# First stage of a one-core diffusion backbone step: six column chunks instead of four, its last block run in the main loop

## The chip, the cores and the metric

The kernel runs on one core of one Trainium2 chip. The metric is the device time of one execution, in microseconds (us), lower is better. Engines: TensorE (PE, matmuls; PEld is its weight load), VectorE (DVE), ScalarE (ACT), GpSimd (POOL) and SyncE (SP, which only issues DMAs here). A dense matmul's 512 columns can start every 0.23 us at TensorE's upper clock and every 0.43 us at half of it.

## What is computed

One layer over 128 context tokens and 128 latent tokens (streams s = 0 and 1), model width 2048, float32:

```python
mods = silu(c) @ w_ada + b_ada            # shift1, scale1, gate1, shift2, scale2, gate2, per stream
h = rmsnorm(x, norm1_g) * (1 + scale1) + shift1
p = h @ w_in + b_in                       # u_fourier (1024) | q | k | v (1024 each) | gate_A | gate_B (2048 each)
a = fourier_mix(p.u_fourier) @ w_fourier
b = attention(p.q, p.k, p.v, cached keys and values, bias) @ w_na_o     # 8 heads of 128
x = x + gate1 * ((sigmoid(p.gate_A) * a + sigmoid(p.gate_B) * b) @ w_out)
h2 = rmsnorm(x, norm2_g) * (1 + scale2) + shift2
x = x + gate2 * hier_moe(h2)              # 16 experts of hidden width 512, two per token
y = rmsnorm(x, final_norm_g)              # also returned: k and v of the context tokens
```

## The kernel before

**Dense steps.** All dense weights stream in 96 steps `l` of 1 MB each (512 rows by 512 columns: LOAD_K = 4 slices of 128 rows). Such a load goes into a ring `raw` of four slots. ScalarE rounds it to `w_hi` (`high`, L1309) and VectorE takes the rest, `w_lo` (`low`, L1663), in two half loads, called units. Each unit is 12 matmuls on TensorE (`unit`, L759 to L761: hi by hi, hi by lo, lo by hi, two row slices, two streams). There are four slots of `w_hi`/`w_lo` (AHEAD = 4 units), so the conversion of a unit waits until the unit four before it has been used, and a ring slot comes free when both of its halves have been converted.

**adaLN rows.** `w_ada` is 96 MB. The shift1 and scale1 columns (32 MB) are taken in four blocks of 512 columns. A block is eight loads of 1 MB into a ring `araw` of four slots, each used by one `ada_block` (16 matmuls, L722). When the eight are in, ScalarE copies the sums to `modrow` (`evac_block_rows`, L1361), TensorE turns them (`mod_block`, L777), VectorE finishes `mod` (L1713, L1715), and both modulate and split four slices of h (`modulate`, `split_h`, `h_ready`). The other four vectors (64 MB) come as 64 "supers" through the ring `raw`, each used by one `ada_super` (L738). SP issues all these loads from one queue, in the order of use; a load that waits for its slot holds up everything behind it.

**First stage.** A slice of h is ready only after its adaLN block. So steps 0 to 15 run block by block: block b of four applies the rows of h that it has just got to P0_CHUNKS = 4 column chunks of `w_in`, and VectorE adds each result to the sum in SBUF (`add_partial`, L1745). Between the units TensorE runs the next block's `ada_block`s: two after unit 0, one after 1, two after 2, one after 3, two after 4, then half of unit 5, `mod_block`, the other half, and units 6 and 7. In the last block it runs supers 0 to 4 there. ScalarE, in program order, does `high` of the next block's first unit, then `evac_block_rows`, then `modulate`.

**Main loop.** Steps 16 to 95: the other four chunks of q, k, v and u (to L_MERGE = 32), the gates with `w_na_o` and `w_fourier` (to L_OUT = 80), and `w_out`. One super runs in each step after its first unit, up to step 69; the last five come at the end. Beside them run the eight attention heads, one every two steps from step 17 (HEAD_AT): `head_transposes` (L862, L865) at HEAD_AT, `scores` (L871 to L873) one step later, `transpose_probs` (L881) two and `probs_values` three steps later. The transposes of a head's cached keys wait until VectorE has scaled the scores of the head before (`scale_scores`, L1893 to L1899, `scores_ready`), since both use PSUM bank 6. The cached keys and values have two slots in `cst`: POOL loads head h when head h - 2 is done. POOL loads the attention bias (written to DRAM and read back skewed), and the DFT constants, once all four blocks of h are ready (`h_ready` 8).

**Experts.** After step 95 come routing and the 16 experts, 192 MB of weights in a ring of eleven slots; a first few of these loads start as the dense ring comes free.

## Time and profile before

| | |
|---|---|
| Median of 3 runs | 1247.66 us (1242.78, 1247.66, 1248.76) |
| The profiled execution's own time | 1242.94 us |
| Its span | 1241.1 us |
| TensorE busy | 1151.5 us, 93% |
| DMA | 424.33 MB, mean 342 GB/s |

The profile is of one execution. Its rows are given below in groups. Times in them are us from the start of the span, so a row's place can be compared with the stages: the first adaLN block up to 40.9 us, the four blocks of the first stage up to about 176.5 us, the main loop up to about 745 us, routing and experts to the end. A matmul's duration is modelled to its end and overlaps the next one's start; the steps between starts tell the pace.

### The profile page before, as it was taken

The numbers are of one execution on the slowest core, as the hardware profiler recorded it, in microseconds if no ns is written. First come the engines' busy times: TensorE is split into PE (matmuls) and PEld (weight loads), VectorE is DVE, ScalarE is ACT, GpSimd is POOL, SyncE is SP. The second block draws the span as 40 slices with busy tenths as digits, with TensorE's granted clock in tenths as the row PEclk, the third lists the DMA queues.
The fourth block names the chain that finished last, engine by engine and source line by source line (L and its number), as shares of the span: only waits on it lengthen the run. The fifth ranks groups of instructions, "written<-read, shape, count | busy, mean of one in ns | idle before, by whom it ended". The sixth has DMA issues, their size and how long they took to land.

```text
span 1241.1 us, 14456 instructions
## 1 busy us (share of the span) xinstructions
PE 1151.5 (93%) x5593; PEld 685.3 (55%) x5593; DVE 529.9 (43%) x760; ACT 368.6 (30%) x516; POOL 45.4 (4%) x83
## 2 busy tenths in 40 slices
PE   4899989999999999999999999999998989888785
PEld 2556657776756666767887774444343334333232
DVE  0355545555434445455565546125233232414046
ACT  3323323443333333333445534222011011201013
POOL 0000210010000300000000000000000000000000
PEclk9899999999999999999999999999999999999998
DMA  9999898887767998888675559999999999999998
GB/s 358 387 383 383 306 356 313 286 315 274 257 212 273 302 335 318 313 314 306 201 251 188 203 191 424 395 423 423 422 423 424 423 424 422 422 423 424 423 413 344
DMA packets 114404, 424.33 MB, mean 342 GB/s; under 512 B 8912, under 2 KB 9088, under 8 KB 81440
## 3 DMA queue, kind: packets, MB, share of 16 engines
q1 hardware_dynamic: 109600, 411.59, 86.5%
q0 software_dynamic: 4144, 11.22, 2.7%
q8 instruction: 45, 0.74, 0.2%
q10 hardware_dynamic: 592, 0.59, 0.1%
q14 instruction: 23, 0.19, 0.0%
HBM read 419.42 MB, written 3.95 MB: 341 GB/s over the span
## 4 chain that ended last, share of the span: by engine, by line
PE 68%; DMA 28%; DVE 1%; issue 1%; SPq 1%; ACT 1%; POOL 0%; DVEq 0%
PE bank L759 14%; PE bank L761 13%; PE bank L760 13%; PE bank L1138 10%; DMA mraw<-in_w_exp_up 6%; PE bank L738 4%; DMA raw<-in_w_in 3%; DMA mraw<-in_w_exp_gate 3%; PE bank L1168 3%; DMA raw<-in_w_ada 2%; PE bank L1079 2%; DMA araw<-in_w_ada 2%; DMA mraw_y<-in_w_exp_gate 2%; DMA mraw_g<-in_w_exp_up 2%; DMA mraw_x<-in_w_exp_up 2%; DMA mraw_g<-in_w_exp_down 2%
## 5 line engine op out<-in xcount | busy, mean ns | idle before, releaser
L1663 DVE TENSOR_TENSOR w_lo<-raw,w_hi 128x1024 fp32r<-128x1024 f32 x192 | 233.7, 1224 | 268.4 <-ACT w_hi L1309 268.0
L1309 ACT ACTIVATE w_hi<-raw 128x1024 fp32r<-128x1024 f32 x192 | 202.2, 1058 | 323.8 <-PE bank L761 233.0
L759 PE MATMUL bank<-w_hi,h_hi 128*128 128x512 f32 x512 | 212.5, 415 | 2.5 <-DVE w_lo L1663 2.5
L1138 PE MATMUL bank<-mraw,xg 128*64 128x512 f32 x768 | 193.6, 602 | 15.8 <-DMA mraw<-in_w_exp_gate 7.8
L761 PE MATMUL bank<-w_hi,h_lo 128*128 128x512 f32 x512 | 202.4, 395 | 0.0
L760 PE MATMUL bank<-w_lo,h_hi 128*128 128x512 f32 x512 | 202.3, 395 | 0.0
L1138 PEld LDWEIGHTS bank<-mraw,xg 128*64 128x64 f32 x768 | 61.8, 137 | 118.2 <-issue 113.9
L759 PEld LDWEIGHTS bank<-w_hi,h_hi 128*128 128x128 f32 x512 | 97.8, 191 | 53.0 <-issue 34.7
L761 PEld LDWEIGHTS bank<-w_hi,h_lo 128*128 128x128 f32 x512 | 97.5, 190 | 21.8
L760 PEld LDWEIGHTS bank<-w_lo,h_hi 128*128 128x128 f32 x512 | 97.8, 191 | 19.3 <-issue 1.0
L1168 PE MATMUL bank<-mraw,hidT 128*64 128x512 f32 x320 | 83.3, 596 | 16.1 <-DMA mraw<-in_w_exp_down 13.7
L2104 DVE SCALAR_TENSOR_TENSOR d_lo<-bank,slot_w,d_hi 128x512 fp32r<-128x512 f32 x32 | 24.0, 748 | 160.5 <-ACT d_hi L1609 159.8
L1609 ACT ACTIVATE d_hi<-bank,slot_w 128x512 fp32r<-128x512 f32 x32 | 22.0, 687 | 229.6 <-PE bank L1168 142.2
L2116 DVE TENSOR_TENSOR bank<-bank,ga2b 128x512 f32<-128x512 f32 x64 | 41.5, 694 | 79.6 <-PE bank L1209 79.5
L738 PE MATMUL bank<-raw,cpad 128*32 128x512 f32 x512 | 68.0, 604 | 5.6 <-DMA raw<-in_w_ada 5.6
L1168 PEld LDWEIGHTS bank<-mraw,hidT 128*64 128x64 f32 x320 | 26.7, 136 | 60.4 <-issue 56.0
L722 PE MATMUL bank<-araw,cpad 128*32 128x512 f32 x256 | 34.8, 640 | 18.7 <-DMA araw<-in_w_ada 18.7
L759 PE MATMUL bank<-w_hi,m_hi 128*128 128x512 f32 x128 | 51.5, 402 | 0.0
L761 PE MATMUL bank<-w_hi,m_lo 128*128 128x512 f32 x128 | 50.0, 391 | 0.0
L760 PE MATMUL bank<-w_lo,m_hi 128*128 128x512 f32 x128 | 49.9, 390 | 0.0
L2051 DVE TENSOR_TENSOR xg<-bank,rbi 128x512 f32<-128x512 f32 x32 | 21.9, 686 | 53.0 <-PE bank L1079 52.5
L1138 PE MATMUL bank<-mraw_x,xg 128*64 128x512 f32 x88 | 40.0, 597 | 2.1 <-DMA mraw_y<-in_w_exp_gate 1.7
(277 smaller groups left out, 1305.0 us busy)
## 6 DMA issues: line engine op xcount, KB each, us to landing
raw<-in_w_in SPq DMA_DIRECT2D x64, 1024.0 KB, 5.6
raw<-in_w_ada SPq DMA_DIRECT2D x64, 1024.0 KB, 7.3
mraw<-in_w_exp_up SPq DMA_DIRECT2D x51, 1024.0 KB, 20.9
mraw<-in_w_exp_gate SPq DMA_DIRECT2D x49, 1024.0 KB, 20.9
mraw<-in_w_exp_down SPq DMA_DIRECT2D x40, 1024.0 KB, 20.8
araw<-in_w_ada SPq DMA_DIRECT2D x64, 512.0 KB, 10.0
raw<-in_w_out SPq DMA_DIRECT2D x16, 1024.0 KB, 5.1
raw<-in_w_na_o SPq DMA_DIRECT2D x8, 1024.0 KB, 5.2
```

The source lines that it names most:

```text
L722: last = nc.tensor.matmul(bank[7 - b % 2][32 * g:32 * g + 32], cpad[:, 2 * j + g % 2], araw[:, n % ARAW, g], start=j == 0, stop=j == 7)
L738: last = nc.tensor.matmul(bank[7][32 * g:32 * g + 32], cpad[:, k], raw[:, n % RAW, g], start=k == 0, stop=k == KD - 1)
L759: nc.tensor.matmul(o, hi[:, k, s], wh, start=k == first, stop=False)
L760: nc.tensor.matmul(o, hi[:, k, s], wl, start=False, stop=False)
L761: last = nc.tensor.matmul(o, lo[:, k, s], wh, start=False, stop=k == final)
L1079: last = nc.tensor.matmul(out[:, kk * EPG * CAP:(kk + 1) * EPG * CAP], (t_hi, t_lo)[part][:, s, k * P:(k + 1) * P], pick[:, s, g * EPG:(g ...
L1138: last = nc.tensor.matmul(out[x * CAP:(x + 1) * CAP], xg[:, q * LOAD_K + kk, e * CAP:(e + 1) * CAP], slab(slot)[:, kk * COL:(kk + 1) * COL ...
L1168: last = nc.tensor.matmul(bank[first_bank + n][x * CAP:(x + 1) * CAP], hidT[:, i % 2, k, x * CAP:(x + 1) * CAP], slab(slot)[:, n * COL:(n ...
L1309: nc.scalar.activation(w_hi[:, u % AHEAD], r, ACT.Copy).then_inc(hi_ready, 1)
L1663: v.tensor_tensor(w_lo[:, u % AHEAD], r, w_hi[:, u % AHEAD].bitcast(F32), ALU.subtract).then_inc(raw_done[n % RAW], 4)
L2104: v.scalar_tensor_tensor(out=d_lo[:, c % 2], in0=bank[first_bank + n][:], scalar=slot_w[:, i:i + 1], in1=d_hi[:, c % 2].bitcast(F32), op0= ...
L2116: v.tensor_tensor(bank[out + s][:], bank[out + s][:], ga2b[:, s, cols], ALU.mult).then_inc(y_scaled, 1)
```

## The change

P0_CHUNKS goes from 4 to 6, so that q, k and v are all in the first stage. Only three of its blocks (steps 0 to 17) stay in the block loop; the fourth (steps 18 to 23) is run by the main loop, which now starts at L_LOOP = 18 and also carries the supers from super 0 on: two in step 18, then one in each step up to step 76. L_MERGE, L_OUT and L_ALL stay 32, 80 and 96. In the block loop one `ada_block` follows each of the units 0 to 7 of a block's twelve, and `mod_block` stands behind unit 8. In SP's order the super loads stand one step further ahead of the dense loads, and are used with a lead of one step in the new numbering. The heads start at steps 21, 23, 24, 26, 28, 29, 31 and 33, `cst` has four slots, ScalarE's exponentials wait for the transposes of the head before, and POOL loads four heads and six bias rows first, then the attention bias once three blocks of h are ready.

```diff
@@ -200,3 +200,3 @@
         mb = place("mb", [P, NS, COL], B + 4 * KB)
-        cst = place("cst", [P, 2, 2, HD], B + 8 * KB)
+        cst = place("cst", [P, 4, 2, HD], B + 4 * KB)
         qkT = place("qkT", [P, 4, TOK], B + 10 * KB)
@@ -333,3 +333,4 @@
-        P0_CHUNKS, BLOCKS = 4, 4
+        P0_CHUNKS, BLOCKS = 6, 4
+        L_LOOP = P0_CHUNKS * (BLOCKS - 1)
         L_MAIN = 4 * P0_CHUNKS
@@ -339,4 +340,3 @@
         A_SUPER = 32
-        A_MAIN = A_SUPER + 3
-        L_LAST_ADA = L_MAIN + 96 - A_MAIN
+        L_LAST_ADA = L_LOOP + 96 - A_SUPER
         LATE_ADA = 5
@@ -345,5 +345,5 @@
-        ring_order = ["dense"] * (L_MAIN - 3) + ["ada", "dense"] * 3
-        for l in range(L_MAIN, L_ALL):
-            ring_order += ["ada", "dense"] if l < L_LAST_ADA - LATE_ADA else ["dense"]
+        ring_order = ["dense"] * (L_LOOP + 1)
+        for l in range(L_LOOP, L_ALL):
+            ring_order += ["ada"] * (l < L_LAST_ADA - LATE_ADA) + ["dense"] * (l + 1 < L_ALL)
         ring_order += ["ada"] * LATE_ADA
@@ -363,3 +363,3 @@
-        ADA_LEAD = 2
+        ADA_LEAD = 1
@@ -367,3 +367,8 @@
-            return L_MAIN + 16 * (super_chunk - GATE1) + 15 + A_SUPER - A_MAIN - ADA_LEAD
+            return L_LOOP + 16 * (super_chunk - GATE1) + 15 - ADA_LEAD
+
+        def supers_at(l):
+
+            first, last = l + ADA_LEAD * (l > L_LOOP), l + ADA_LEAD
+            return [A_SUPER + i - L_LOOP for i in range(first, last + 1) if i < L_LAST_ADA - LATE_ADA]
@@ -395,3 +400,3 @@
-        HEAD_AT = [L_MAIN + 1 + 2 * h for h in range(8)]
+        HEAD_AT = [L_LOOP + i for i in (3, 5, 6, 8, 10, 11, 13, 15)]
         DFT_AT = HEAD_AT[7] + 2
@@ -485,13 +490,12 @@
             for b in range(1, BLOCKS):
-                for i in range(4):
-                    ada_block_load(b, 2 * i)
-                    ada_block_load(b, 2 * i + 1)
+                for i in range(P0_CHUNKS):
+                    if i < 4:
+                        ada_block_load(b, 2 * i)
+                        ada_block_load(b, 2 * i + 1)
                     dense_load(P0_CHUNKS * (b - 1) + i + 1)
-            for i in range(3):
-                ada_super_load(A_SUPER + i)
-                dense_load(L_MAIN - 3 + i)
-            for l in range(L_MAIN, L_ALL):
+            for l in range(L_LOOP, L_ALL):
                 if l < L_LAST_ADA - LATE_ADA:
-                    ada_super_load(A_MAIN + l - L_MAIN)
-                dense_load(l)
+                    ada_super_load(A_SUPER + l - L_LOOP)
+                if l + 1 < L_ALL:
+                    dense_load(l + 1)
@@ -633,6 +637,6 @@
-                if h >= 2:
-                    pool.wait_ge(pv_done, h - 1)
-                pool.dma_start(cst[:, h % 2, 0:1], kc_v[:, h:h + 1, :]).then_inc(ctx_landed[h % 2], 16)
-                pool.dma_start(cst[:, h % 2, 1:2], vc_v[:, h:h + 1, :]).then_inc(ctx_landed[h % 2], 16)
+                if h >= 4:
+                    pool.wait_ge(pv_done, h - 3)
+                pool.dma_start(cst[:, h % 4, 0:1], kc_v[:, h:h + 1, :]).then_inc(ctx_landed[h % 4], 16)
+                pool.dma_start(cst[:, h % 4, 1:2], vc_v[:, h:h + 1, :]).then_inc(ctx_landed[h % 4], 16)
@@ -645,10 +649,10 @@
             pool.wait_ge(xT_ready, 6)
-            load_bin(0)
-            load_bin(1)
-            load_bin(2)
-            load_bin(3)
-            pool.wait_ge(h_ready, 8)
-            load_bias_rows()
             load_cached_head(0)
             load_cached_head(1)
+            load_cached_head(2)
+            load_cached_head(3)
+            for n in range(6):
+                load_bin(n)
+            pool.wait_ge(h_ready, 6)
+            load_bias_rows()
             skew_bias_rows()
@@ -656,9 +660,3 @@
             pool.dma_start(cst_all[:, C_DFTN:C_MASK], constants[:, C_DFTN:C_MASK]).then_inc(consts_in, 16)
-            load_bin(4)
-            load_bin(5)
-            load_cached_head(2)
-            load_cached_head(3)
             load_bin(6)
-            load_cached_head(4)
-            load_cached_head(5)
             load_bin(7)
@@ -669,6 +667,8 @@
                                uqkv[:, 0, FW + (1 + n) * NA:FW + (2 + n) * NA]).then_inc(kv_sent, 16)
-            gate1_bias_row()
-            load_bin(8)
+            load_cached_head(4)
+            load_cached_head(5)
             load_cached_head(6)
+            load_bin(8)
             load_cached_head(7)
+            gate1_bias_row()
             load_bin(9)
@@ -741,3 +741,3 @@
-            def unit(l, half, within=None):
+            def unit(l, half):
@@ -753,4 +753,2 @@
                     k = LOAD_K * quad + UNIT_K * half + t
-                    if t and within is not None:
-                        mod_block(within)
                     wh, wl = w_hi[:, u % AHEAD, t], w_lo[:, u % AHEAD, t]
@@ -817,34 +815,16 @@
-            def next_ada(b, js):
-
-                for j in js:
-                    if b < BLOCKS:
-                        ada_block(b, j)
-                    else:
-                        ada_super(A_SUPER + j)
-
-            for b in range(BLOCKS):
-                l = P0_CHUNKS * b
-                last_block = b == BLOCKS - 1
+            for b in range(BLOCKS - 1):
+                u = 2 * P0_CHUNKS * b
                 pe.wait_ge(h_ready, 2 * b + 2)
-                banks_free(l)
-                unit(l, 0)
-                next_ada(b + 1, (0,) if last_block else (0, 1))
-                unit(l, 1)
-                next_ada(b + 1, () if last_block else (2,))
-                banks_free(l + 1)
-                if b == 0:
-                    pe.wait_ge(xT_ready, 8)
-                unit(l + 1, 0)
-                next_ada(b + 1, (1,) if last_block else (3, 4))
-                unit(l + 1, 1)
-                next_ada(b + 1, () if last_block else (5,))
-                banks_free(l + 2)
-                unit(l + 2, 0)
-                next_ada(b + 1, (2, 3) if last_block else (6, 7))
-                unit(l + 2, 1, None if last_block else b + 1)
-                banks_free(l + 3)
-                unit(l + 3, 0)
-                next_ada(b + 1, (4,) if last_block else ())
-                unit(l + 3, 1)
+                for n in range(2 * P0_CHUNKS):
+                    if n % 2 == 0:
+                        banks_free(u // 2 + n // 2)
+                    if b == 0 and n == 2:
+                        pe.wait_ge(xT_ready, 8)
+                    unit(u // 2 + n // 2, n % 2)
+                    if n == 8:
+                        mod_block(b + 1)
+                    if n < 8:
+                        ada_block(b + 1, n)
+            pe.wait_ge(h_ready, 2 * BLOCKS)
@@ -852,3 +832,3 @@
-                j = h % 2
+                j = h % 4
                 if h == 0:
@@ -858,3 +838,3 @@
                     pe.wait_ge(chunk_read, reads(5))
-                pe.wait_ge(ctx_landed[j], (h // 2 + 1) * 32)
+                pe.wait_ge(ctx_landed[j], (h // 4 + 1) * 32)
                 for m in range(4):
@@ -888,3 +868,3 @@
                 nc.tensor.matmul(bank[5][:, 0:P], uqkv[:, 0, at:at + HD], prT[:, 0], start=True, stop=True)
-                nc.tensor.matmul(bank[5][:, P:2 * P], cst[:, h % 2, 1], prT[:, 1], start=True, stop=False)
+                nc.tensor.matmul(bank[5][:, P:2 * P], cst[:, h % 4, 1], prT[:, 1], start=True, stop=False)
                 nc.tensor.matmul(bank[5][:, P:2 * P], uqkv[:, 1, at:at + HD], prT[:, 2], start=False, stop=True
@@ -984,3 +964,3 @@
-            for l in range(L_MAIN, L_ALL):
+            for l in range(L_LOOP, L_ALL):
                 banks_free(l)
@@ -993,4 +973,4 @@
                 unit(l, 0)
-                if l + ADA_LEAD < L_LAST_ADA - LATE_ADA:
-                    ada_super(A_MAIN + l + ADA_LEAD - L_MAIN)
+                for a in supers_at(l)[:1]:
+                    ada_super(a)
                 if l == L_ALL - 3:
@@ -1020,2 +1000,4 @@
                 unit(l, 1)
+                for a in supers_at(l)[1:]:
+                    ada_super(a)
                 if l > L_OUT and l % 4 == 0:
@@ -1380,6 +1362,4 @@
                     transposed(7)
-                for n in range(2, 2 * P0_CHUNKS):
+                for n in range(2, 2 * P0_CHUNKS if b < BLOCKS - 1 else AHEAD):
                     high(u + n)
-            for u in range(2 * L_MAIN, 2 * L_MAIN + AHEAD):
-                high(u)
@@ -1413,2 +1393,4 @@
                 act.wait_ge(scores_ready, h + 1)
+                if h:
+                    act.wait_ge(prT_done, h)
                 nc.scalar.activation(prb[:, 0], scr[:, 0], ACT.Exp, bias=smx[:, 0:1], accum_out=smx[:, 2:3])
@@ -1482,3 +1464,3 @@
-            for l in range(L_MAIN, L_ALL):
+            for l in range(L_LOOP, L_ALL):
                 if l == L_OUT:
@@ -1865,3 +1847,3 @@
                     low(1)
-                for ch in range(1, P0_CHUNKS):
+                for ch in range(1, P0_CHUNKS if b < BLOCKS - 1 else AHEAD // 2):
                     low(2 * (l + ch))
@@ -1870,7 +1852,2 @@
                         add_partial(l + ch - 2)
-            low(2 * L_MAIN)
-            low(2 * L_MAIN + 1)
-            add_partial(L_MAIN - 2)
-            low(2 * L_MAIN + 2)
-            low(2 * L_MAIN + 3)
@@ -1934,9 +1911,9 @@
-            for l in range(L_MAIN, L_ALL + 1):
+            for l in range(L_LOOP, L_ALL + 1):
-                if l == L_MAIN + 1:
+                if l == L_LOOP + 1:
                     add_mask()
-                if l == L_MAIN:
-                    add_partial(L_MAIN - 1)
-                else:
+                if L_LOOP < l <= L_MAIN:
+                    add_partial(l - 1)
+                elif l > L_MAIN:
                     chunk, quad, quads = chunk_of(l - 1)
@@ -1976,3 +1953,3 @@
                     logit_constants()
-                if l == L_MERGE - 1:
+                if l == L_MERGE + 2:
                     dve.wait_ge(bias_row_in, 32)
```

(A line that only declares four `ctx_landed` semaphores instead of two is left out.)

## Rows read from the trace of the kernel before

**Rows 1.** Page: busy time of the engines over the span
```profile
PE 1151.5 (93%) x5593; PEld 685.3 (55%) x5593; DVE 529.9 (43%) x760; ACT 368.6 (30%) x516; POOL 45.4 (4%) x83
```

**Rows 2.** Stretches by stage: length, busy us of each engine (instructions), clock, DMA, GB/s
```profile
40.86:79.26 38.40, 36.23 (x168) 22.18 (x169) 17.63 (x25) 10.75 (x14) 1.07 (x2) 0.88 1.05 387
79.26:112.30 33.04, 31.64 (x169) 19.89 (x169) 17.84 (x26) 10.66 (x14) 0.00 (x0) 1.00 1.05 383
112.30:145.35 33.05, 32.04 (x164) 20.05 (x163) 17.93 (x26) 10.53 (x13) 2.73 (x6) 0.95 0.94 350
145.35:176.50 31.15, 29.26 (x144) 19.69 (x143) 14.33 (x16) 7.29 (x8) 9.99 (x17) 1.00 0.95 306
186.50:745.00 558.50, 556.79 (x2702) 405.81 (x2701) 281.34 (x349) 220.95 (x278) 28.47 (x49) 1.00 0.77 270
745.00:1241.10 496.10, 437.50 (x2090) 181.73 (x2087) 169.74 (x296) 89.74 (x165) 0.00 (x0) 0.99 1.00 416
```

**Rows 3.** TensorE in order of time: a pair of ada_blocks, one between two units
```profile
55.19 1.92 PE L722 MATMUL bank<-araw,cpad 128*32 128x512 f32 x16
...
59.72 0.39 PE L761 MATMUL bank<-w_hi,h_lo 128*128 128x512 f32 x1
60.03 1.06 PE L722 MATMUL bank<-araw,cpad 128*32 128x512 f32 x8
61.03 0.50 PE L759 MATMUL bank<-w_hi,h_hi 128*128 128x512 f32 x1
61.37 0.39 PE L760 MATMUL bank<-w_lo,h_hi 128*128 128x512 f32 x1
```

**Rows 4.** Waits, 41 to 190 us: total us, times, longest
```profile
PE bank L738 <- DMA raw<-in_w_ada: 4.4, 3, 2.5
PE bank L777 <- ACT modrow L1361: 2.4, 2, 1.4
PE bank L722 <- DMA araw<-in_w_ada: 2.1, 2, 1.8
```

**Rows 5.** Waits, 200 to 745 us, same columns
```profile
PE bank L862 <- DMA cst<-in_cache_v_ctx: 1.7, 2, 1.1
```

**Rows 6.** TensorE in order of time: five starts after idle (in brackets)
```profile
67.18 1.94 PE L722 MATMUL bank<-araw,cpad 128*32 128x512 f32 x8 [1.78 <-DMA araw<-in_w_ada]
104.63 1.06 PE L777 MATMUL bank<-cst_all,modrow 128*128 128x4 f32 x8 [1.40 <-ACT modrow L1361]
137.39 1.05 PE L777 MATMUL bank<-cst_all,modrow 128*128 128x4 f32 x8 [1.01 <-ACT modrow L1361]
172.72 1.06 PE L738 MATMUL bank<-raw,cpad 128*32 128x512 f32 x8 [1.55 <-DMA raw<-in_w_ada]
181.94 1.06 PE L738 MATMUL bank<-raw,cpad 128*32 128x512 f32 x8 [2.49 <-DMA raw<-in_w_ada]
```

**Rows 7.** Stretches around three of them, columns of rows 2
```profile
64.00:71.00 7.00, 4.93 (x23) 1.93 (x22) 1.68 (x3) 1.13 (x2) 0.54 (x1) 0.76 1.05 386
136.00:144.00 8.00, 6.99 (x28) 5.43 (x27) 6.50 (x14) 4.04 (x7) 1.38 (x3) 0.79 0.78 305
179.00:187.00 8.00, 5.51 (x21) 3.41 (x21) 5.05 (x6) 3.06 (x3) 0.00 (x0) 0.79 1.01 396
```

**Rows 8.** ScalarE in order of time, before the third mod_block
```profile
103.03 1.06 ACT L1309 ACTIVATE w_hi<-raw 128x1024 fp32r<-128x1024 f32 x1 [6.11 <-DMA raw<-in_w_in]
104.00 0.58 ACT L1361 ACTIVATE modrow<-bank 128x512 f32<-128x512 f32 x1
```

**Rows 9.** One head's scores: last pair of matmuls, first and last VectorE step
```profile
214.41 0.39 PE L873 MATMUL bank<-qkT 128*128 128x128 f32 x2
...
214.84 0.42 DVE L1893 TENSOR_SCALAR scr<-bank 128x256 f32<-128x256 f32 x1 [2.02 <-PE bank L873]
...
215.94 0.42 DVE L1899 TENSOR_REDUCE smx<-scr 128x1 f32<-128x256 f32 x1
```

**Rows 10.** Chain that ended last: one transfer of the fourth block
```profile
165.59 16.30 DMA raw<-in_w_ada
```

6 lines of the change are left out of this document (3 added, 3 removed).

## The prediction

> **What bounds the kernel now.** I read the engines' busy time first: TensorE is busy 93% of the span [rows 1]. An average over stages can't say where a change pays, so I cut the span into stages [rows 2]. From 745 us to the end the DMA share is 1.00 at 416 GB/s: the experts are bound by their loads, and whatever the change saves or costs before 745 us moves that part as a whole, one to one. From 186.5 to 745 us TensorE is busy 556.8 of 558.5 us at full clock, with the DMA at 0.77: that part is TensorE's. The first stage is the surprise. Its DMA share is 0.94 to 1.05, which looks like a stage bound by transfers, but TensorE too is busy 36.2 of 38.4, 31.6 of 33.0, 32.0 of 33.1 and 29.3 of 31.2 us. Both are nearly full. TensorE has the same steps and the same adaLN groups to do before 745 us in either kernel, so the change can only win what TensorE now loses in waits and at half clock. I sum that first, then what is added.
>
> **What it removes.** The waits of TensorE in the first stage are 4.4 us for supers, 2.4 us for `modrow` and 2.1 us for adaLN blocks [rows 4]; two heads wait 1.7 us for cached values [rows 5]. Idle time counts from a modelled end: a matmul is given 0.39 us, and the next starts 0.23 us after it, so each wait costs 0.16 us more, less the 0.08 us seam that any inserted group has [rows 3]. For nine waits: 10.6 + 0.7 = 11.3 us. Then the clock. Behind three of the waits TensorE ran at 1.2 GHz: the granted clock is 0.76 of 7 us, 0.79 of 8 and 0.79 of 8 [rows 7], each time about 3.4 us at half clock, or 1.7 us lost; the first of them lies partly in the idle time, so 4.7 us for the three. Sum: 16.0 us. Part by part the reasons go away:
> - The adaLN blocks came too fast: eight in 5 units, where one load takes 2.7 us (1.05 MB at 387 GB/s). After, eight are spread over 8 units.
> - The supers of the fourth block waited because POOL's small transfers (bias, DFT constants) ran beside them; one load took 16.3 us [rows 10]. These transfers now fall in block 2. A block there moves 14 MB, 38 us at 385 GB/s, beside about 45 us of TensorE (below), so 7 us of slack take up the 5 us or so that they cost; I read that from the fourth block's 306 GB/s over 31 us against 387 [rows 2], part of which was a ring that stood still.
> - Cached heads are loaded four deep. Six of the eight are asked for two steps or more ahead, no longer one.
>
> **What it adds.** (a) *Single adaLN groups.* A single group takes 60.03 to 61.03 and its seams, 59.72 to 61.37 less two plain steps of 0.23: 1.19 us. A pair lasts 1.92 where one lasts 1.06, so the second costs 0.86 where a group of its own costs 1.19 [rows 3]. Each pair split costs 0.33 us; three pairs in three blocks and one of supers make 3.3 us.
> (b) *The mod wait.* `mod_block` now stands directly behind unit 8. In ScalarE's order the row copy follows `high` of the next block's first unit, and that needs the slot of unit 8 itself. So TensorE waits for: the end of unit 8 to reach ScalarE (0.2 us: 0.16 to the modelled end and 0.04, the hop of 214.80 to 214.84 [rows 9]), `high` until the copy starts 0.97 us, and the copy until the matmuls start 0.63 us [rows 6, 8]. That is 1.8 us against a seam of 0.08: 1.7 us a block, 5.2 us for three. Before, two adaLN groups and half a unit covered it. Behind `mod_block`, units 9 to 11 (8.2 us) cover modulation.
> (c) *Adjacent heads.* Heads 1 and 2, and 4 and 5, are one step apart. In that step TensorE does the scores of one and then the transposes of the other, whose last waits for `scores_ready`. The last pair of the scores starts at 214.41 and ends, as modelled, at 214.80, so TensorE could go on at about 214.55; VectorE's chain ends at 216.36 [rows 9], 1.8 us later. Three or four tenths go to the four transposes that need not wait (two such 128-column matmuls are the pair of 0.39). I take 1.5 us, twice: 3.0 us; bounds 1.4 and 1.8 each.
> (d) *Head 0* at step 21 needs chunk 2, whose sum VectorE makes only in that step, after `high` and `low` of unit 45: 0.2 + 1.06 + 1.23 + 1.28 = 3.8 us, as much as a unit and a super: 0.2 us.
> (e) *Clock.* Of five waits of 1.0 to 2.5 us three were followed by half clock (1.78, 1.01, 2.49), two were not (1.40, 1.55) [rows 6, 7]: their stretches show a granted clock of 1.00 [rows 2]. The new waits show as idle of 1.6 us, thrice. I take a half: 3 x 0.5 x 1.7 = 2.6 us. Bounds: none, 0; all five waits, 8.5.
> (f) *Transfers that come late after all.* In block 0 the last adaLN load lands at 67.2 [rows 6]; three dense loads and 0.5 MB of cached heads behind it end near 77.5, about when unit 8 does (40.86, one unit at half clock, eight more units, eight groups: 77.4). I take 0.5 us; bounds 0 and 4.
> Eight more partial sums of 1.28 us on VectorE lie under its load of 54% (17.8 of 33.0 us) [rows 2] and cost nothing; if `low` became late they would show as waits of L759.
>
> **Sum.** 3.3 + 5.2 + 3.0 + 0.2 + 2.6 + 0.5 = 14.8 added, 16.0 removed: 1.2 us faster. Against the profiled execution's own 1242.94 that is 1241.7; it lies 4.7 us below the median of the runs, so for the median I say 1246.4. With the low bounds (clock 0, lateness 0) it is 4.3 us faster; with the high ones 8 us slower. About 0.5%, 6 us, is what a measurement of this kernel can tell from no change.
>
> The Trainium skill, TensorE: Matmul & The Clock Gate (What's actually happening), says the array's clock is throttled by default and released by activity. By that rule waits this short between busy stretches ought to leave the clock up, and the sum would be 3.8 us faster. The trace disagrees at 67.18 and 137.39, so the measurement decides.
>
> **Rivals.**
> *Faster: the stage is bound by transfers.* If TensorE's time in the first stage were free, steps moved there would be hidden. The loads up to step 18 end six loads (16 us) after 145.4; 78 steps and 59 supers are then left instead of 79.5 and 58 at 186.5. That gives about 25 us, 1223 us. For it: the DMA share of 1.0. Against it: TensorE's 32 of 33 us. A milder form keeps (a) and (c) but finds the mod wait and the clock covered: 16.0 - 7.0 = 9 us, 1239. It needs `modrow` ready within a seam of unit 8, which the order on ScalarE excludes unless unit 8's slot was free earlier. Chance of the two: 0.15. The Trainium skill, Perfetto Trace Analysis (Optimization Strategy), advises interleaving regimes whose most-contended engines differ; by that rule the first form would hold. The trace shows both engines full here, not one.
> *Slower: the load of the next block's first unit gates the adaLN row.* ScalarE's `high` ahead of the copy waited 6.11 us for its transfer, until 103.03 [rows 8]. That load is now the last of four dense ones behind the adaLN block. If it lands 3 us after unit 8 in each block, TensorE waits 3 us more thrice and drops to half clock each time: 9 + 2.5 = 11.5 us more, 1258 us. It decides where the transfer lands later than unit 8's end. For it: block 0's margin is nil. Against it: blocks 1 and 2 have 7 us. Chance 0.13.
> *The stalls stay.* If the fourth block's supers still wait (6 us with their clock), since super 2's slot comes free only one step before its use, the result is 5 us slower, 1252.5. Chance 0.12, still within 0.5%.
>
> **How the numbers follow.** My forecast has 0.6. Its own range is 1243 to 1252. Faster by over 0.5% comes from the first rival: 0.15. Slower by over 0.5% comes from the second and from the upper tail of clock and lateness: 0.15. The rest, 0.7, is within 0.5%. For 8 in 10 the range reaches to 1239 and to 1254.
>
> **What would show it.** Right: first-stage blocks of about 45 us with TensorE near full and a DMA share below 1; L777 waiting thrice for `modrow`, each near 1.6 us idle; no waits of L738 and L722 for transfers beyond a few tenths; step 18 starting near 178 us; L865 idle about 1.3 us twice, in steps 24 and 29; the main loop ending within 3 us of 745. Wrong: L777 waits of 3 us or more, w_hi before them waiting for DMA; L738 waits in steps 18 to 20; or blocks much shorter than 45 us, which would mean that I overcounted TensorE's work.

## The result, and the profile after

The changed kernel takes 1253.39 us (median of 7 runs, 1249.64 to 1256.27), the kernel before 1246.64 (7 runs beside them, 1242.78 to 1248.76). The ratio is 1.0058, 95% interval 1.0037 to 1.0080: slower by 6.75 us, where 1.2 us faster was forecast. The time lies inside the range of 1239 to 1254, but outside the 1243 to 1252 that I gave my own forecast, and the interval excludes both "no change" and the direction that I forecast: I had given 0.15 to "slower by over 0.5%". The cause that I had priced at 0.5 us turned out to be the largest term of the account below.

The profiled execution after is that of 1256.27 us, the slowest of its seven (span 1254.5); the one before, 1242.94, was among the fastest. So the two profiles lie 13.4 us apart where the medians lie 6.75 apart, and I check what I read in them on a control run further down.

The page after, busy time of the engines [rows 1], and then the stretches: blocks 1, 2 and 3 of the first stage, the main loop, the experts. Columns as in [rows 2]: length, busy us of PE, PEld, DVE, ACT and POOL with their instructions, granted clock, DMA share, GB/s.

```profile
PE 1160.6 (93%) x5593; PEld 687.7 (55%) x5593; DVE 536.4 (43%) x772; ACT 369.2 (29%) x516; POOL 45.6 (4%) x83
```

```profile
40.84:90.45 49.61, 46.64 (x217) 30.23 (x218) 24.67 (x33) 15.36 (x18) 2.15 (x4) 0.94 1.05 384
90.45:137.39 46.94, 45.25 (x217) 29.61 (x216) 25.04 (x34) 14.64 (x17) 5.13 (x10) 0.96 0.94 338
137.39:195.30 57.91, 49.26 (x217) 32.57 (x216) 25.12 (x34) 14.62 (x17) 5.53 (x8) 0.88 0.77 251
195.30:755.00 559.70, 557.22 (x2715) 400.88 (x2717) 284.25 (x356) 218.26 (x275) 25.45 (x43) 1.00 0.77 274
755.00:1254.50 499.50, 441.69 (x2098) 183.53 (x2093) 170.77 (x297) 90.76 (x166) 0.00 (x0) 0.98 1.00 414
```

Three blocks do the same work in 49.6, 46.9 and 57.9 us; about 45 was forecast. The third stands out three times over: TensorE idle for 8.7 us, the clock at 0.88, and the DMA share down to 0.77 with 251 GB/s, though loads are what it will turn out to wait for. From there to the experts TensorE is busy 557.2 of 559.7 us, as before.

The waits of TensorE after (what waited for what: us in total, times, longest), from 41 to 190 us and, the last row, from 190 to 760 us. They answer to [rows 4] and [rows 5].

```profile
PE bank L757 <- DVE uqkv L1727: 8.1, 3, 7.0
PE bank L775 <- ACT modrow L1343: 5.1, 3, 1.7
...
PE bank L845 <- DVEq L1878: 2.5, 2, 1.2
```

Every wait of [rows 4] and [rows 5] that was to go is gone: no super, no adaLN block and no cached value is waited for. The `modrow` wait and the adjacent heads came as forecast. The row left out, 2.5 us for `w_lo`, is the start of the first block at 40.8 us; the kernel before has the same one, 2.5 us, and every run further down has one of 1.8 to 3.4 us there, which I leave out too. One row is new: TensorE waits 7.0 us once for VectorE to empty a PSUM bank of partial sums. TensorE's instructions at the four longest idle times (in brackets, idle before and what ended it), and the one behind the longest:

```profile
81.26 1.05 PE L775 MATMUL bank<-cst_all,modrow 128*128 128x4 f32 x8 [1.69 <-ACT modrow L1343]
...
126.59 1.05 PE L775 MATMUL bank<-cst_all,modrow 128*128 128x4 f32 x8 [1.69 <-ACT modrow L1343]
...
167.96 0.80 PE L757 MATMUL bank<-w_hi,h_hi 128*128 128x512 f32 x1 [6.96 <-DVE uqkv L1727]
168.56 0.63 PE L758 MATMUL bank<-w_lo,h_hi 128*128 128x512 f32 x1
...
182.90 1.57 PE L775 MATMUL bank<-cst_all,modrow 128*128 128x4 f32 x8 [1.69 <-ACT modrow L1343]
```

A partial sum takes VectorE 1.28 us, so it is not slow; it is late. The chain of work that ended last, from 140 to 175 us (start, us, what), says why:

```profile
146.80 16.36 DMA raw<-in_w_in
...
163.19 1.06 ACT w_hi L1291
...
164.35 0.90 DVE w_lo L1645
165.49 1.22 DVE w_lo L1645
166.71 1.21 DVE uqkv L1727 x2
```

The partial sum stands behind `low` of the next unit pair in VectorE's order, `low` waits for `high` on ScalarE (idle 17.88 us before 163.19), and `high` waits for one dense load of 1 MB that was issued at 146.80 and took 16.36 us. Its neighbours in SP's queue (start, us the issue took, transfers), POOL's transfers, and the stretches just before and during the load:

```profile
141.33 5.06 SPq L460 DMA_DIRECT2D araw<-in_w_ada  x4
146.80 0.81 SPq L484 DMA_DIRECT2D raw<-in_w_in  x1
149.22 9.41 SPq L460 DMA_DIRECT2D araw<-in_w_ada  x4
```

```profile
139.44 1.15 POOL L612 DMA_DIRECT2D bias_rows<-rpbpad  x1 [2.48 <-DMA rpbpad<-in_rpb]
...
147.94 2.82 POOL L621 DMA_DIRECT2D bias<-bias_rows  x4 [7.36 <-DMA bias_rows<-rpbpad]
150.75 0.57 POOL L660 DMA_DIRECT2D cst_all<-shape_constants  x1
151.32 1.08 POOL L634 DMA_DIRECT2D bin<-in_b_in  x2
```

```profile
135.00:140.00 5.00, 5.00 (x24) 4.03 (x22) 2.41 (x4) 2.05 (x2) 2.52 (x5) 1.00 0.37 97
147.00:163.00 16.00, 14.00 (x74) 7.78 (x72) 0.84 (x2) 0.00 (x0) 4.38 (x7) 1.00 1.01 323
```

So two things meet. From 135 to 140 us the DMA engines ran at a share of 0.37, with 97 GB/s: they had time to spare, but the dense load could not use it, since in SP's one queue it stands behind adaLN loads, and these wait for their slots: SP stood still for 15.7 us, until 141.33, for the slot that the block's first `ada_block` frees. When it was at last issued it met POOL's bias and constants: 323 GB/s at a share of 1.01, where block 1 had 384 at 1.05. How long such a load takes otherwise (from issue to landing) is in these rows: first the median of the dense loads issued from 60 to 140 us in this kernel, then this same load, at the same place in the queue, in the run a3 below, where POOL's transfers stand elsewhere:

```profile
raw<-in_w_in SPq DMA_DIRECT2D x11, 1024.0 KB, 12.6
```

```profile
raw<-in_w_in SPq DMA_DIRECT2D x1, 1024.0 KB, 8.2
```

Here it took 16.4.

### The profile page after: what moved, and what is told of

The parts are those of the page before. It is cut to its first block, busy times and chain, and to the rows that moved or that the text cites. A ratio compares the mean times of both kernels' runs of the same rounds, so it can differ in the third digit from the quotient of the medians.

```text
span 1254.5 us, 14486 instructions
## 1 busy us (share of the span) xinstructions
PE 1160.6 (93%) x5593; PEld 687.7 (55%) x5593; DVE 536.4 (43%) x772; ACT 369.2 (29%) x516; POOL 45.6 (4%) x83
## 4 chain that ended last, share of the span: by engine, by line
PE 72%; DMA 24%; DVE 2%; issue 1%; SPq 1%; ACT 1%; DVEq 0%; ACTq 0%
PE bank L757 15%; PE bank L759 14%; PE bank L758 14%; PE bank L1120 10%; DMA mraw<-in_w_exp_up 6%; PE bank L738 5%; DMA mraw<-in_w_exp_gate 3%; PE bank L1150 3%; DMA raw<-in_w_in 2%; PE bank L1061 2%; DMA araw<-in_w_ada 2%; DMA mraw_x<-in_w_exp_up 2%; DMA mraw_y<-in_w_exp_gate 2%; DMA mraw_g<-in_w_exp_down 2%; DMA mraw_g<-in_w_exp_up 2%; DMA mraw_y<-in_w_exp_up 2%
## 5 line engine op out<-in xcount | busy, mean ns | idle before, releaser
L757 PE MATMUL bank<-w_hi,h_hi 128*128 128x512 f32 x512 | 214.0, 418 | 10.8 <-DVE uqkv L1727 8.1
L759 PE MATMUL bank<-w_hi,h_lo 128*128 128x512 f32 x512 | 203.5, 397 | 0.0
L758 PE MATMUL bank<-w_lo,h_hi 128*128 128x512 f32 x512 | 203.1, 397 | 0.0
L757 PEld LDWEIGHTS bank<-w_hi,h_hi 128*128 128x128 f32 x512 | 98.4, 192 | 70.9 <-issue 40.1
L759 PEld LDWEIGHTS bank<-w_hi,h_lo 128*128 128x128 f32 x512 | 98.1, 192 | 22.3
L758 PEld LDWEIGHTS bank<-w_lo,h_hi 128*128 128x128 f32 x512 | 98.6, 193 | 18.6 <-issue 0.2
L1150 PE MATMUL bank<-mraw,hidT 128*64 128x512 f32 x320 | 83.3, 596 | 16.4 <-DMA mraw<-in_w_exp_down 14.0
L757 PE MATMUL bank<-w_hi,m_hi 128*128 128x512 f32 x128 | 51.4, 402 | 0.0
L722 PE MATMUL bank<-araw,cpad 128*32 128x512 f32 x256 | 35.7, 631 | 16.6 <-DMA araw<-in_w_ada 16.6
L759 PE MATMUL bank<-w_hi,m_lo 128*128 128x512 f32 x128 | 50.0, 391 | 0.0
L758 PE MATMUL bank<-w_lo,m_hi 128*128 128x512 f32 x128 | 49.9, 390 | 0.0
```

The costliest lines, as they stand in the source:

```text
L722: last = nc.tensor.matmul(bank[7 - b % 2][32 * g:32 * g + 32], cpad[:, 2 * j + g % 2], araw[:, n % ARAW, g], start=j == 0, stop=j == 7)
L757: nc.tensor.matmul(o, hi[:, k, s], wh, start=k == first, stop=False)
L758: nc.tensor.matmul(o, hi[:, k, s], wl, start=False, stop=False)
L759: last = nc.tensor.matmul(o, lo[:, k, s], wh, start=False, stop=k == final)
L1150: last = nc.tensor.matmul(bank[first_bank + n][x * CAP:(x + 1) * CAP], hidT[:, i % 2, k, x * CAP:(x + 1) * CAP], slab(slot)[:, n * COL:(n ...
```

## The experiments

The theory: the loss is (1) that late dense load, (2) the `modrow` wait of 1.69 us thrice with the half clock behind it. The rivals: single adaLN groups (seams) cost more than I took; POOL's transfers alone are at fault and would have to be moved; or the loss is an accident of one profile. Each edit is against the kernel after, but the last. Medians, ratios to the kernel before run beside them, and the loss by clock, (1 − mean granted clock) x span, as the mean over all runs of that kernel (before stands once for each batch; the first figures belong to a0, a1, a4 and a3, the second to a6, a2, a9 and a8, the third to a5, a10, a11 and b1; where kernels of two batches are compared, I compare their distances from before). The ratio on record isn't the quotient of these two medians: for a10 it is 0.9900 against 0.9916, for a5 1.0010 against 1.0022. So a distance in us is good to 1 or 2 us, no better. Where an edit adds a line, L757, L722 and L775 appear as L758, L723 and L776 in the rows:

| kernel | median us (runs) | ratio to before, 95% | to before, us | clock loss, us |
|---|---|---|---|---|
| before (three batches) | 1245.04, 1245.63, 1246.46 (33, 20, 23) | | | 18.1, 16.4, 18.1 |
| a0 after again | 1252.07 (10) | 1.0066 (1.0045, 1.0087) | +7.0 | 20.3 |
| a1 mod one unit later | 1244.71 (12) | 0.9994 (0.9976, 1.0012) | −0.3 | 16.3 |
| a4 dense load first | 1246.77 (12) | 1.0016 (1.0001, 1.0032) | +1.7 | 18.3 |
| a3 POOL's transfers later | 1248.07 (12) | 1.0012 (0.9995, 1.0030) | +3.0 | 16.5 |
| a6 POOL's transfers earlier | 1251.50 (11) | 1.0047 (1.0032, 1.0062) | +5.9 | 18.7 |
| a5 partial sum first | 1249.25 (12) | 1.0010 (0.9993, 1.0027) | +2.8 | 18.1 |
| a2 adaLN groups in pairs | 1251.30 (10) | 1.0039 (1.0017, 1.0062) | +5.7 | 20.2 |
| a9 = a1 + a4 | 1236.03 (6) | 0.9922 (0.9897, 0.9946) | −9.6 | 11.1 |
| a8 = a1 + a2 + a4 + a6 | 1238.21 (6) | 0.9934 (0.9912, 0.9957) | −7.4 | 14.6 |
| a10 = a9, constants late | 1236.01 (6) | 0.9900 (0.9875, 0.9924) | −10.5 | 13.2 |
| a11 = a1 + a4 + a6 | 1236.48 (6) | 0.9907 (0.9883, 0.9931) | −10.0 | 12.6 |
| b1 before, POOL earlier | 1247.62 (12) | 1.0005 (0.9987, 1.0023) | +1.2 | 18.3 |

**a0, the kernel after once more.**

> The changed kernel again, unaltered, as the control of its neighbours. Theory P (POOL's small transfers of the third block, 139 to 161 us, delay one dense load by 16 us; TensorE waits 7 us for it through VectorE's partial sum): this wait is of L757 for VectorE's partial sum at about 168 us and comes back here within 3 us of its size, and the time is 5 to 8 us above the kernel before. Theory B (transfers are simply too many, 14 MB a block): waits for transfers or partial sums show in all three blocks. Theory N (the profiled execution was an odd one): no wait over 2 us, and the time is within 4 us of the kernel before.

1252.07 us, ratio 1.0066: the loss is there again. Its waits, 41 to 200 us, and its span:

```profile
PE bank L757 <- DVE uqkv L1727: 7.7, 4, 4.5
PE bank L775 <- ACT modrow L1343: 5.1, 3, 1.7
```

```profile
core 0: 1250.1 us, clock 0.985
```

The same two causes with almost the same sums (8.1 and 5.1 above), so the loss isn't an accident of one profile. The late load's largest piece was 4.5 us here, 6.96 there. POOL issued its bias blocks at 150.41 here, 2.5 us later than there; this load took 12.9 us, and the next dense one, issued at 153.94, took 17.3 and has 1.3 us of the 7.7.

**a1, the modulation one unit later.** Nothing is left out; `mod_block` gets one unit between the row copy's release and itself.

```diff
-                    if n == 8:
+                    if n == 9:
                         mod_block(b + 1)
```

> Only mod_block moved from behind unit 8 to behind unit 9. Theory M (the copy of the adaLN rows can start only when unit 8 has freed its slot, so TensorE idles 1.7 us thrice and may fall to half clock behind it): the three waits of mod_block for modrow go from 1.69 us each to below 0.1, half-clock stretches behind them go, and the time falls 5 to 9 us below a0_after. Theory M-hidden (another wait, of units 0 and 1 of the next block for h_ready, takes its place since only units 10 and 11 are left, 5.5 us, for a chain of 4 us and more): less than 2 us gained.

1244.71 us, 7.4 us less than a0. The L775 wait is gone from the list, while the other stays (9.2 us, its longest 7.2 at 162.47):

```profile
PE bank L757 <- DVE uqkv L1727: 9.2, 3, 7.2
```

5.1 us is the wait itself, and the loss by clock falls from 20.3 to 16.3 us, 4.0 more. Against these the wait for the late load is 1.5 us longer, as is to be expected where TensorE comes to it sooner. That makes 7.6, about the 7.4 measured.

**a4, the dense load issued ahead of the adaLN loads of its place.**

```diff
                 for i in range(P0_CHUNKS):
+                    dense_load(P0_CHUNKS * (b - 1) + i + 1)
                     if i < 4:
                         ada_block_load(b, 2 * i)
                         ada_block_load(b, 2 * i + 1)
-                    dense_load(P0_CHUNKS * (b - 1) + i + 1)
```

> Only SP's order changed in the block loop: each dense load stands ahead of the two adaLN loads instead of behind them, so it no longer waits for their slots. Theory Q (the load was late because it was issued late, queued behind adaLN loads whose slots come free only as TensorE uses them; its own slot was free 20 us before): with POOL's transfers where they are, the wait of L757 at 168 us goes, and the two small ones of the first block (0.3 and 0.9 us) too: 6 to 10 us below a0_after. Theory P alone (bandwidth taken by POOL): part of the wait stays, as a wait of L722 for its adaLN load, 2 to 6 us.

1246.77 us, 5.3 us less than a0:

```profile
PE bank L775 <- ACT modrow L1343: 5.8, 3, 2.4
...
PE bank L722 <- DMA araw<-in_w_ada: 2.5, 2, 1.8
```

No wait for partial sums is left: theory Q, though the gain is a little under its 6 to 10 us. What is late next are adaLN loads (2.5 us in two pieces; the later one, issued at 149.90, took 16.11 us), and one `modrow` wait grew to 2.4.

**a3, POOL's bias and constants moved behind the first stage.**

```diff
             load_bias_rows()
+            pool.wait_ge(unit_used, 2 * L_LOOP - 2)
             skew_bias_rows()
             load_bias_blocks()
-            pool.dma_start(cst_all[:, C_DFTN:C_MASK], ...)
...
             load_cached_head(5)
+            pool.dma_start(cst_all[:, C_DFTN:C_MASK], ...)
...
-                if l == L_LOOP + 1:
+                if l == HEAD_AT[0] + 1:
                     add_mask()
```

> Only POOL's small transfers moved: the bias goes to DRAM and back from the last steps of the third block on, the DFT constants after the k and v output, and VectorE adds the mask in step 22. Theory P: the 7 us wait of L757 at about 168 us goes (at most 1 us is left), with the half clock behind it (2.5 us): 6 to 9 us below a0_after. Theory B: the dense load is late all the same, and the time stays within 3 us of a0_after. A third outcome: the supers of steps 18 to 24 or the first head wait for the transfers now, as in the kernel before, 2 to 6 us.

1248.07 us, 4.0 us less than a0. The order of SP's queue is the one of a0, and still the large wait is gone:

```profile
PE bank L776 <- ACT modrow L1344: 5.1, 3, 1.7
PE bank L739 <- DMA raw<-in_w_ada: 2.0, 1, 2.0
...
PE bank L758 <- DVE uqkv L1728: 1.9, 2, 1.1
```

So the 16.36 us need POOL's transfers beside them: the same load took 8.2 us, and TensorE was busy without a gap from 147 to 163 us. But these transfers now meet the supers: 2.0 us at 197.00 and 1.2 more at 204.95. That is the wait of [rows 4] again, which the change had removed.

**a6, the same transfers moved forward, into the time around 118 us,** behind `h_ready` 4 and the first units of block 2.

```diff
-            pool.wait_ge(h_ready, 6)
+            pool.wait_ge(h_ready, 4)
             load_bias_rows()
+            pool.wait_ge(unit_used, 2 * P0_CHUNKS)
             skew_bias_rows()
             load_bias_blocks()
```

(The constants are moved as in a3.)

> POOL's transfers earlier instead of later: the bias goes to DRAM from the first unit of the second block on (about 93 us), where the trace shows the DMA share fall to 0.5 while SP waits for an adaLN slot, and the DFT constants after the k and v output. Theory P: the same gain as with late transfers, without the waits of the supers: no wait of L757 over 1.5 us in the third block, 4 to 7 us below the unaltered changed kernel (1252.1), so 1245 to 1248. Theory Q (the late issue alone decides): a dense load of the second block is late now, the wait returns there, and the time stays within 2 us of 1252.

1251.50 us, 1.1 us nearer to before than a0, which their intervals don't tell apart. The gain that theory P had forecast didn't come; it is theory Q's outcome. The wait has moved one block forward, most of it in one piece:

```profile
PE bank L758 <- DVE uqkv L1728: 7.8, 5, 5.3
```

```profile
122.38 0.80 PE L758 MATMUL bank<-w_hi,h_hi 128*128 128x512 f32 x1 [5.34 <-DVE uqkv L1728]
```

**a5, the partial sum ahead of `low` in VectorE's order.**

```diff
                 for ch in range(1, ...):
-                    low(2 * (l + ch))
-                    low(2 * (l + ch) + 1)
                     if ch >= 2:
                         add_partial(l + ch - 2)
+                    low(2 * (l + ch))
+                    low(2 * (l + ch) + 1)
```

> The changed kernel with VectorE's partial sum ahead of the two halves of low in the block loop, instead of behind them. Theory O (order on VectorE): TensorE waited for a PSUM bank whose sum was ready to be taken, but queued behind the conversion of a late load; now only the load itself is waited for, as a wait of L757 for w_lo: the 7 us become 4 to 5, the small ones of the first block go: 2 to 4 us below the unaltered changed kernel (1252.1). Theory Q (the late load alone): the wait keeps its size under another name, and the time stays within 1.5 us.

1249.25 us, 4.2 us nearer to before than a0 (2.8 against 7.0):

```profile
162.61 0.47 PE L757 MATMUL bank<-w_hi,h_hi 128*128 128x512 f32 x1 [1.17 <-DVE w_lo L1645]
...
173.55 0.76 PE L757 MATMUL bank<-w_hi,h_hi 128*128 128x512 f32 x1 [2.92 <-DVE w_lo L1645]
```

TensorE now waits for the weights of the late load itself, later and for less: 4.1 us in two pieces in place of 6.96 in one. The order on VectorE charged the load to TensorE a unit pair early. It isn't why the load was late, but it is a third condition of the loss: undone alone, it gives back as much as a3.

**a2, two adaLN groups behind units 0, 2, 4 and 6.**

```diff
-                    if n < 8:
+                    if n < 8 and n % 2 == 0:
                         ada_block(b + 1, n)
+                        ada_block(b + 1, n + 1)
```

> Only the adaLN groups of the block loop are put together again, two after each of units 0, 2, 4 and 6. The seam theory: 12 pairs save 0.33 us each, 4.0 us: L722 takes 1.86 us a pair, and the blocks last 1.3 us less each. Rival: the last group comes one unit earlier but mod_block stays behind unit 8, so nothing else moves, yet the adaLN loads are wanted earlier in pairs: waits of L722 for its load of 1 us and more take the gain back, less than 2 us gained.

1251.30 us, 1.3 us nearer to before than a0, again within the intervals. The seams are saved, but TensorE then reaches the same late load sooner and waits longer (9.6 us, longest 6.6, where a0 had 7.7 and 4.5):

```profile
PE bank L757 <- DVE uqkv L1728: 9.6, 4, 6.6
```

**a9, both mends that paid: a1 and a4.**

> mod_block behind unit 9 and dense loads ahead of the adaLN loads. If the two losses are separate (7.4 us and 5.3 us as measured alone), the sum is 12.7 us below 1252.1: 1239 to 1241, some 5 us below the kernel before. If they share a cause (the clock falls once whichever wait comes first, or the freed wait only moves the lateness), less than 9.5 us: 1242.5 or more.

1236.03 us, ratio 0.9922: 9.6 us faster than the kernel before and 16.6 better than a0, by their distances from before. Both theories of the expectation put it higher. Waits from 41 to 200 us, span, and two stretches about as long as blocks:

```profile
PE bank L722 <- DMA araw<-in_w_ada: 3.9, 2, 3.2
```

```profile
core 0: 1233.9 us, clock 0.991
```

```profile
88.00:132.00 44.00, 44.00 (x220) 29.14 (x219) 25.83 (x37) 14.62 (x17) 3.23 (x7) 1.00 1.05 387
132.00:180.00 48.00, 44.76 (x216) 29.50 (x215) 24.80 (x35) 14.52 (x17) 7.39 (x12) 0.96 0.87 289
```

The middle block is full: 44.00 of 44.00 us, clock 1.00, DMA 1.05. From the first adaLN group of this block (89.45) to that of the next (132.80) it takes 43.4 us: the block of 45 us that I had forecast for all three, less its mod wait. The single mends give 7.4 + 5.3 = 12.7 us, together they give 16.6. Four kernels enter that surplus of 4.0 us, each with an interval of 2 to 3 us to either side, so it may be chance. The clock has a part of the surplus: measured from before in the same batch, a0 loses 2.2 us more by clock, a1 1.8 less and a4 0.2 more, so singly 4.0 and 2.0 us are won; a9 loses 5.3 less, which is 7.5 won. That is 1.5 of the 4.0 us; the rest I can't place.

**a8, a9 with pairs and the earlier POOL transfers.**

> mod_block behind unit 9, dense loads first, adaLN groups in pairs and POOL's transfers in the gap of the second block. If TensorE's work is the floor of the first stage and all waits go: 7.4 + 5.3 + 4.0 + 2 (the 0.7 and 1.8 us adaLN waits left in a4_dense_first) = 18 us below 1252.1, 1234. If adaLN loads become the bound when the groups come in pairs: waits of L722 over 1 us in the first block, 1238 or more. Either is below the kernel before (1245.0).

1238.21 us: not better than a9. Pairs ask for two adaLN loads at once, and L723 waits for them six times:

```profile
PE bank L723 <- DMA araw<-in_w_ada: 6.8, 6, 2.9
```

a11 below is a8 without its pairs; it is 2.6 us further below before, though the intervals of the two overlap.

**a10 and a11, a9 with only the constants moved, or with the bias earlier as well.**

> a9_mod9_dense with the DFT constants moved behind the k and v output. The 3.2 us wait of an adaLN group at 160 us in a9 stands beside three POOL transfers: the bias to DRAM, back, and the constants with two bias rows. If the constants make it, the wait falls below 1.5 us and the time by 2 us, to 1234; if the bias does, the time stays at 1236 within 1 us.

> a8_all without its pairs, that is a9_mod9_dense with POOL's transfers in the second block. If the pairs cost a8_all its 2 us (adaLN loads wanted earlier than they land), this kernel is at 1236 or below, with waits of L722's line of 2 us at most. If the earlier transfers do, it is at 1238 and the 2.9 us wait near 118 us stays.

1236.01 and 1236.48 us, ratios 0.9900 and 0.9907: neither can be told from a9. One adaLN wait of 2.3 us at 159.06 is what is left in a10, two of 3.1 us in all, 2.5 of it at 115.60, in a11. With both mends in place, where POOL's transfers fall hardly matters.

**b1, the kernel before with its bias transfers earlier** (behind `h_ready` 6). It asks whether that kernel was open to the same collision.

```diff
-            pool.wait_ge(h_ready, 8)
+            pool.wait_ge(h_ready, 6)
             load_bias_rows()
-            load_cached_head(0)
-            load_cached_head(1)
             skew_bias_rows()
...
+            pool.wait_ge(h_ready, 8)
+            load_cached_head(0)
+            load_cached_head(1)
```

> The kernel before with POOL's bias and DFT transfers started after three blocks of h, as the change does, instead of four. Theory R (the four-chunk block order was just as open to a late load, and only the time of POOL's transfers saved it): a dense load of the last block or of the block before it is late, a wait of L759 for a partial sum or w_lo of 2 us and more appears, and the time does not fall below the kernel before although its super waits (4.4 us) shrink. Theory S (its dense loads are issued early enough): the super waits shrink and the time falls 2 to 6 us.

1247.62 us, no difference that can be measured, as theory R has it, but the load that is late is an adaLN load and not the dense one that it named. Waits from 41 to 200 us, and the largest:

```profile
PE bank L723 <- DMA araw<-in_w_ada: 9.7, 5, 6.4
...
PE bank L739 <- DMA raw<-in_w_ada: 0.9, 1, 0.9
```

```profile
143.70 1.94 PE L723 MATMUL bank<-araw,cpad 128*32 128x512 f32 x8 [6.41 <-DMA araw<-in_w_ada]
```

The supers' wait shrinks from 4.4 us [rows 4] to 0.9, and an adaLN load that is 6.4 us late takes its place. With the loads in their old order, one was late wherever I put these transfers: in the second block (a6), the third (the kernel after, b1) or the fourth (the kernel before, a3).

## Why the prediction was wrong

Up to the same sixteen matmuls behind step 95 (741.42 us before, 752.59 after) the profiles differ by 11.2 us, where the medians differ by 6.75. Term by term against the forecast, for these two profiles:

- **Removed, 16.0 us.** The waits of 11.3 us are gone, and so are the three half clocks of [rows 7], as those. Right.
- **(a) Single groups, 3.3 us.** At 105.10 the period from one single group to the next is 3.94 us, of which 2.72 are the unit: 1.22 for the group and its seams, against 1.19. Right. That pairs win nothing back (a2) is not that seams cost nothing: waits for partial sums grew (9.6 us against 7.7 in a0).
- **(b) Mod wait, 5.2 us.** 1.69 us idle three times, 5.1 in all. Right in size and place, and a1 shows it: with one unit more between, it is gone. The 45 us that I gave a block hold this wait too, as the 43.4 us of a9's show.
- **(c) Adjacent heads, 3.0 us.** 1.24 us idle twice, 2.5. Right. **(d)** right: nothing shows.
- **(e) Clock, 2.6 us; measured about 7.6.** This term was mis-sized. The stretches of the profile after, in the columns from above:

```profile
78.00:86.00 8.00, 6.31 (x32) 5.04 (x32) 6.59 (x14) 3.99 (x7) 0.54 (x1) 1.00 1.05 386
124.00:132.00 8.00, 6.31 (x25) 4.84 (x25) 5.67 (x13) 3.19 (x6) 0.17 (x1) 0.79 1.05 387
158.00:176.00 18.00, 11.04 (x45) 6.90 (x44) 7.08 (x9) 5.07 (x5) 0.00 (x0) 0.81 1.05 390
180.00:188.00 8.00, 6.31 (x23) 5.00 (x22) 5.36 (x13) 3.19 (x6) 0.00 (x0) 0.70 0.42 148
188.00:196.00 8.00, 8.00 (x32) 6.46 (x31) 3.25 (x5) 2.60 (x3) 0.00 (x0) 0.87 0.30 95
```

  The clock stayed up after the mod wait at 81.26 and fell to 1.2 GHz after the same wait of 1.69 us at 126.59 (0.21 x 8 = 1.7 us lost) and at 182.90 (0.30 x 8 + 0.13 x 8 = 3.4 us). Behind the 6.96 us of the late load matmuls came every 0.43 us in place of 0.23 (168.56 to 169.84) until about 173, some 2.5 us. Two of three was more than my "a half", one of the two lasted twice as long as I took, and the third piece hung on a wait I hadn't foreseen. More profiles say that two of three is the better figure: seven have these mod waits (after, a0 and a2 to a6), and in the stretch of 8 us around each the granted clock was 0.65 to 0.79 for 15 of the 21 waits and 1.00 for 6. The value lies within my bounds of 0 and 8.5. The runs give the term without one odd profile: I had 4.7 us of clock removed and 2.6 added, 2.1 us less; by the table a0 loses 2.2 us more than before, so over the runs this sum was 4.3 us too low.
- **(f) Transfers that come late after all, 0.5 us; measured 8.1**, twice my upper bound of 4. This is the step that failed, and with it its ground under "What it removes": "These transfers now fall in block 2 ... so 7 us of slack take up the 5 us or so that they cost". The partial sums, which I had put at nothing, carry part of it: the wait came by the very sign I had named for them (the first line of a unit, L759 before and L757 after), and a5 gives 4.2 us back by their order alone.

With those two sizes, and 2.6 for (c), the sum is 3.3 + 5.2 + 2.6 + 0.2 + 7.6 + 8.1 = 27.0 added, 16.0 removed: 11.0 us slower, against 11.2 measured. The other 2.2 us between the spans lie behind that point, in one execution each, and I can't tell them from the spread of the runs.

That fit is of a slow execution of the one kernel with a fast one of the other. a0's profile, nearer to the medians, has the same sixteen matmuls at 748.77, 7.3 us behind before. Its waits are as long (7.7 and 5.1 us), and its clock cost less: 0.79, 1.00 and 0.79 of 8 us around the mod waits and 0.86 of 12 us behind the late load, 5.0 us, and 1.6 us less than in either of the two profiles at the start of the first block (0.79 of 8 us against 0.58 and 0.59). With these the sum is 24.0 added, 17.6 removed, 6.4 us. So both terms stand in a usual execution, (e) with a smaller size.

What was wrong with the 7 us? The figure itself wasn't. A block does have more of TensorE's time than of transfer time; the share of 0.77 and the 97 GB/s in front of the load show that the DMA engines did stand idle. I took the slack of a whole block for the lead of each load in it. But the loads are issued in one order, each when the slot of the one ahead is free, so idle DMA time ahead of a stuck load can't be used, and a collision hits with the lead that the load had when issued. This one's lead can be read: TensorE stood still from 161.00 (167.96 less 6.96), and from landing to partial sum the chain takes 4.80 us (163.16 to 167.96), so the load had to land by 156.2, 9.4 us after its issue. It took 16.36; in a3, without POOL's transfers, its 8.2 us kept that time with 1.2 us to spare, and the 12.6 us of the usual dense load would not have. I searched block 0 alone for lateness because there the margin by sums was nil; block 0 showed 0.86 us at most. Three things meet in this wait, and each of three runs takes one away: a4 the issue order (the wait goes, 5.3 us), a3 POOL's transfers (the wait goes, 4.0 us), a5 the partial sum's place behind `low` (the wait shrinks to 4.1, 4.2 us). a6 and b1 show that the collision goes where the transfers go. The change moved a collision that stood at the supers, at 6 us or so with its clock, to a place where a `low`, a partial sum and then TensorE wait for it.

The rivals: mine on the slower side put the late load ahead of the adaLN row, 3 us in each block. A dense load was late indeed, and the direction was right, but the place wasn't: the row copy never waited more than the 1.69 us of (b). The first stage bound by transfers, the faster rival, is refuted by [rows 2]'s counterpart after: three blocks with 45.3 to 49.3 us of TensorE each, none shorter. Its milder form, with mod wait and clock covered, was forecast at 1239, 9 us below before. `mod_block` one unit later is not enough for it (a1, 0.3 us below before); with the dense loads first as well a9 gets there, 9.6 us below. Of the signs that I named, the mod waits, the heads and the absent waits for transfers came; the blocks of 45 us didn't, step 18 started at 195.3 instead of near 178, and the main loop ended 10 us late. None of my signs of being wrong showed, since the loss came by another way.

The Trainium skill, TensorE: Matmul & The Clock Gate (What's actually happening), says that activity releases the throttle. I had kept its reading against the trace as a sum 3.8 us faster; the traces after refute that sum again, with half clock behind two of its three waits of 1.69 us, and a9, whose middle block has no wait and a clock of 1.00 throughout, is what the rule looks like when it is met.

What stays open: how late that load is varies (4.5, 6.96 and 7.2 us in three profiles with the same order of loads). In a0, the one with 4.5, POOL's bias blocks were issued 2.8 us after the load, in the other two 1.1 and 4.5, so that alone doesn't order them. Nor did I separate how much of the 16.36 us comes from the bias blocks and how much from the constants: a10 moves the constants alone, but behind a9, where neither matters.

## What to carry to other kernels

The slack of a stage is no lead: for every transfer that is to be absorbed, take the load that is next in the queue at that time, when its slot comes free and what stands ahead of it, and set its landing against the first instruction that needs it. When loads for two rings share one queue, issue first the one whose consumer stands in a long chain (here ScalarE, VectorE, partial sum, TensorE); moving that one line was worth 5.3 us, and moving the modulation behind one more unit 7.4. With both, the changed kernel is at 1236.0 us, 0.8% faster than the kernel before. How much of that is the staging's own stays open: SP's order in the kernel before also has each dense load behind adaLN loads, and no run put it first there.

## What was not expected of the hardware

Two equal waits of 1.69 us with the same eight small matmuls behind them were followed by full clock once (81.26) and half clock once (126.59) within one execution, and the third (182.90) by half clock for about twice as long. In a0, a2, a3, a5 and a6 it was the second wait that kept the full clock. An idle time of that size is thus not a price but a risk, of 0 to 3.4 us, and removing it gives back more than its length: a1 won 7.4 us on 5.1 us of waits.

A single 1 MB load took 16.4 us beside POOL's small transfers and 8.2 us, at the same place in the queue, without them. A block's loads together move at 384 GB/s, one of 1.05 MB in every 2.7 us, but that is a pace and no landing time: half of the dense loads from 60 to 140 us took more than 12.6 us. POOL's transfers aren't needed for a long one either: in a5 a dense load issued at 63.23 took 15.24 us while the engines moved 387 GB/s and POOL issued nothing but two bias rows. [rows 10] has the super that took 16.30 us beside the bias and constants.
